# Attention by pairs of heads, scan sums formed by TensorE, and the sine products of the states on GpSimd

## The reference, cut to what matters

```python
# stick-breaking heads
z = jnp.einsum('bhqd,bhkd->bhqk', q_blk, k) * (q_blk.shape[-1] ** -0.5)
log_fail = jnp.where(earlier, jax.nn.log_sigmoid(-z), 0.0)
log_stick = lax.cumsum(log_fail, axis=3, reverse=True) - log_fail
w = jnp.where(earlier, jnp.exp(jax.nn.log_sigmoid(z) + log_stick), 0.0)
# softmax heads
p = jax.nn.softmax(jnp.where(visible, z, -jnp.inf), axis=-1)
# S5
_, _, h_re, h_im = lax.associative_scan(_complex_affine_combine,
    (lam_re, lam_im, bu_re, bu_im), axis=1)
y = einsum('bsgn,gcn->bsgc', h_re, c_re) - einsum('bsgn,gcn->bsgc', h_im, c_im)
y = jax.nn.gelu(y + d_skip * u)
```

## Time and profile before

| | us |
|---|---|
| median of 3 runs | 2449.45 (2447.01 to 2452.51) |
| the profiled execution, its own time | 2445.27 |
| its span, first to last instruction | 2443.3 |
| TensorE busy | 1999.7 (82%) |
| VectorE busy | 800.5 (33%) |
| ScalarE busy | 263.0 (11%) |
| GpSimd busy | 0.2 (0%) |

### The profile page before, as it was taken

The page is one execution under the profiler, slowest core; times in us unless marked ns, Lnnn a source line. Parts: engine busy times, 40 slices in busy tenths (PEclk is TensorE's granted clock), DMA queues, the critical chain, the costliest instruction groups (busy, mean ns, idle before and its releaser), DMA issues.

```text
span 2443.3 us, 28860 instructions
## 1 busy us (share of the span) xinstructions
PE 1999.7 (82%) x12526; PEld 1046.5 (43%) x12526; DVE 800.5 (33%) x1592; ACT 263.0 (11%) x447; POOL 0.2 (0%) x4
## 2 busy tenths in 40 slices
PE   8769675767666759589999944599999999999988
PEld 4658663222222226446767631343433433333322
DVE  1665742333333343632043377310111211121112
ACT  1221110111111110530100000000000000000000
POOL 0000000000000000000000000000000000000000
PEclk9879787887887769689999965799999999999999
DMA  6210005899999982004343200199999999999996
GB/s 241 78 65 4 2 2 210 377 430 431 431 430 432 429 357 103 0 1 190 138 172 138 104 0 0 73 429 430 404 408 405 379 430 430 431 429 429 430 431 258
DMA packets 50981, 645.06 MB, mean 264 GB/s; under 512 B 8192, under 2 KB 10496, under 8 KB 12064
## 3 DMA queue, kind: packets, MB, share of 16 engines
q1 hardware_dynamic: 50848, 643.11, 62.9%
HBM read 642.04 MB, written 1.05 MB: 263 GB/s over the span
## 4 chain that ended last, share of the span: by engine, by line
PE 69%; DVE 13%; DMA 12%; issue 4%; ACT 2%; DVEq 0%; SPq 0%; ACTq 0%
PE ps L765 67%; DMA slot<-in_moe_w_up 12%; DVE xn L1931 2%; DVE hT L1931 1%; PE ps L1308 1%; DVE hT L1935 1%; DVE xn L1972 1%; DVE xn L2929 1%; DVE sca L1931 1%; ACT L1690 1%; PE ps L774 0%; DVE x_sb L1938 0%; DVE xn L1935 0%; DVE BK L1931 0%; PE ps L914 0%
## 5 line engine op out<-in xcount | busy, mean ns | idle before, releaser
L765 PE MATMUL ps<-slot,xgT 128*32 128x512 f32 (+2 forms) x2368 | 408.3, 672 | 75.6 <-issue 41.0
L765 PE MATMUL ps<-hT,slot 128*128 128x256 f32 (+2 forms) x1536 | 316.0, 368 | 3.2 <-DVE hT L1935 3.2
L765 PEld LDWEIGHTS ps<-hT,slot 128*128 128x128 f32 (+2 forms) x1536 | 274.6, 185 | 45.9 <-DVE hT L1935 4.3
L765 PEld LDWEIGHTS ps<-slot,xgT 128*32 128x32 f32 (+2 forms) x2368 | 130.9, 133 | 345.3 <-issue 319.5
L765 PE MATMUL ps<-slot,xgh 128*64 128x512 f32 x1120 | 256.1, 600 | 4.3 <-DVE x_sb L1938 2.2
L765 PE MATMUL ps<-slot,hTs 128*64 128x512 f32 (+2 forms) x1232 | 253.5, 596 | 0.9 <-DVE hTs L2467 0.9
L765 PEld LDWEIGHTS ps<-slot,hTs 128*64 128x64 f32 (+2 forms) x1232 | 80.4, 132 | 166.6 <-issue 166.6
L765 PE MATMUL ps<-slot,hT 128*128 128x512 f32 (+1 forms) x320 | 142.3, 605 | 4.1 <-ACT hT L1690 2.3
L765 PEld LDWEIGHTS ps<-slot,xgh 128*64 128x64 f32 x1120 | 76.6, 137 | 145.9 <-issue 136.0
L765 PE MATMUL ps<-slot,hTq 128*32 128x512 f32 x512 | 93.9, 868 | 25.9 <-issue 25.4
L1931 DVE TENSOR_TENSOR hsb<-ps,sgx 64x512 f32<-64x512 f32 (+2 forms) x56 | 38.8, 693 | 232.0 <-ACT sgx L1690 141.1
(11 more groups left out here) (364 smaller groups left out, 1734.6 us busy)
## 6 DMA issues: line engine op xcount, KB each, us to landing
slot<-in_moe_w_gate SPq DMA_DIRECT2D x88, 2048.0 KB, 15.4
slot<-in_moe_w_up SPq DMA_DIRECT2D x88, 2048.0 KB, 16.7
slot<-in_moe_w_down SPq DMA_DIRECT2D x88, 2048.0 KB, 18.6
slot<-in_dffn_w_gate SPq DMA_DIRECT2D x7, 2048.0 KB, 7.7
slot<-in_dffn_w_up SPq DMA_DIRECT2D x7, 2048.0 KB, 12.5
slot<-in_dffn_w_down SPq DMA_DIRECT2D x7, 2048.0 KB, 7.7
slot<-in_w_in_tiles SPq DMA_DIRECT2D x6, 2048.0 KB, 8.5
slot<-in_att_w_in SPq DMA_DIRECT2D x3, 2048.0 KB, 12.1
```

The costliest lines, as they stand in the source:

```text
L765: return nc.tensor.matmul(o, l, r, start=start, stop=stop)
```

## The change

In attention the loop goes over four pairs of heads. The stick scores of a pair lie in two banks of a ring of their own (`sticks`, which the sums share) and are read there by ScalarE's Abs and by VectorE, without the copy. Every elementwise step of ScalarE and VectorE covers both heads, and the sums are one matmul of 512 columns and two of 256. The latent scores have a ring of two banks (`latents`). Ahead of the loop the order of the projections changes: one `sqk` bank, then the latents with `q_up` and `kv_up`, then three `sqk` banks, the stick scores of pair 0, one bank of values, the transposes of the heads, the latent scores, the second bank of values. ScalarE's copies of the values move behind `root("heads")`.

In S5 the sums of products ahead of the scans are formed by TensorE, in PSUM, by the identity and its negative (`minus`): eight logical matmuls of 128 rows by 256 columns a step. The scans read PSUM and write `scanned`. The states are multiplied by cosine on VectorE and by sine on GpSimd, and the four products of each tile go through TensorE with `cT`, and with `cN` for the negative: eight logical matmuls in place of four. The states' products of step i-1 stand behind the input products of step i on VectorE. `cN` and `minus` are made beside the dense layer by two more instructions.

```diff
+            stick_project(0)
             pe.wait_ge(lat_ready, 1)
...
+            for n in (1, 2, 3):
+                stick_project(n)
...
+            stick_scores(0)
+            values(0)
             pe.wait_ge(heads_ready, 1)
...
+            latent_scores(0)
+            values(1)
...
+            for hp in range(HP):
+                pe.wait_ge(fails, hp + 1)
+                b = sticks.claim(pe, sticks.at[f"sums{hp}"])
+                mm(b[:, :].rearrange("p (h e c) -> p h e c", h=2, e=2), cst("after"),
+                   blocks(lf)[:, :, 0::2, :]).then_inc(sticks.filled, 1)
+                b = sticks.claim(pe, sticks.at[f"sums{hp}"] + 1)
+                middle = b[:, 0:T].rearrange("p (h c) -> p h c", h=2)
+                mm(middle, cst("after"), blocks(lf)[:, :, 1, :], True, False)
+                mm(middle, cst("ones"), blocks(lf)[:, :, 2, :], False, True).then_inc(sticks.filled, 1)
+                if hp + 1 < HP:
+                    stick_scores(hp + 1)
+                    latent_scores(hp + 1)
+                pe.wait_ge(p_ready, hp + 1)
...
+            for hp in range(HP):
+                act.wait_ge(w_arg, hp + 1)
+                f(wT, la, ACT.Exp).then_inc(w_exp, 1)
+                if hp + 1 < HP:
+                    soft(hp + 1)
+                for k in range(2):
+                    empty(pair_item(f"turned{k}", hp), (pTt[:, k, :], lambda b: b[:, 0:3 * P], 1.0))
+                if hp + 1 < HP:
+                    probabilities(hp + 1)
...
+            for hp in range(HP):
+                if hp:
+                    failing(hp)
+                attempts(hp)
+                normalised(hp)
+                if hp + 1 < HP:
+                    latent_max(hp + 1)
+                dve.wait_ge(w_exp, hp + 1)
+                signal(tt(edge(wT), edge(wT), strictly, ALU.mult), w_ready, hp + 1)
...
+            def s5_turned(i):
                 for m in range(2):
+                    bu.landed(pe, bu.at[i] + m)
+                    b = rotated.claim(pe, rotated.at[i] + m)
+                    mm(b[:, 0:T], ident, vst[:, 0, m, 0, :], True, False)
+                    mm(b[:, 0:T], ident, vst[:, 1, m, 1, :], False, True)
+                    mm(b[:, T:2 * T], ident, vst[:, 0, m, 1, :], True, False)
+                    mm(b[:, T:2 * T], minus[:, :], vst[:, 1, m, 0, :], False, True).then_inc(rotated.filled, 1)
...
+            for i in range(9):
+                if i < 8:
+                    s5_turned(i)
+                if i:
+                    s5_out(i - 1)
                 if i < 6:
                     s5_in(i + 2)
...
+        @block.gpsimd
+        def _(pool):
+            for i in range(8):
+                rotated.landed(pool, rotated.at[i] + 1)
+                if i:
+                    pool.wait_ge(s5y.filled, i)
+                for m in range(2):
+                    nc.gpsimd.tensor_tensor(hsin[:, m], scanned[:, m],
+                                            rot[:, 1, 2 * i + m, :].unsqueeze(1).to_broadcast([P, 2, T]),
+                                            ALU.mult).then_inc(s5_hsin, 1)
...
+            for i in range(10):
                 if i < 8:
+                    s5_products(i)
+                if 0 < i < 9:
+                    s5_states(i - 1)
+                if i > 1:
+                    s5_outputs(i - 2)
+                if i < 8:
+                    s5_scan(i)
```

More of the change, by code:

```diff
@@ L609, in either @@
                         packed(x)
-        def scores_item(kind, h):
-            return V.at["heads"] + 3 * h + ("stick", "latent", "sums").index(kind)
         def pair_item(kind, hp):
             return S_.at["pair"] + 4 * hp + ("turned0", "turned1", "stick", "latent").index(kind)
-        def s5_item(kind, i):
-            return V.at["s5"] + (2 * i + max(i - 1, 0) if kind == "in" else (23 if i == 7 else 3 * i + 4))
         def arrived(eng, name):
@@ L1603, in _ @@
             S_.landed(pe, pair_item("latent", HP - 1))
+            sticks.landed(pe, sticks.total - 1)
+            latents.landed(pe, latents.total - 1)
             out_proj(("p0", "p1"), V.at["wout2"])
@@ new lines, in _, with latent_max @@
+            blocks = lambda x: x.rearrange("p h (b c) -> p h b c", b=3)
+            edge = lambda x: blocks(x)[:, :, 0::2, :]
+            strictly = cst("before").unsqueeze(1).unsqueeze(1).to_broadcast([P, 2, 2, P])
+            def latent_max(hp):
+                for k in range(2):
+                    b = latents.take(dve, latents.at[f"s{hp}"] + k)
+                    own(tt(mz[:, k, 0:P], b[:, 0:P], cst("causal")[:, P:2 * P], ALU.add))
+                    tt(mz[:, k, P:3 * P], b[:, P:3 * P], cst("causal"), ALU.add).then_inc(latents.emptied, 1)
+                own.settle()
+                latents.landed(dve, latents.at[f"s{hp}"] + 1)
+                own(vec.tensor_reduce(st[:, 32:34], mz[:, :, 0:P], AXX, ALU.max))
+                own(vec.tensor_reduce(st[:, 34:36], mz[:, :, P:3 * P], AXX, ALU.max))
+                own.settle()
+                signal(ts(st[:, 36:40], st[:, 32:36], -(MQK ** -0.5), ALU.mult), maxed, hp + 1)
@@ new lines, in failing @@
+            def failing(hp):
+                dve.wait_ge(z_soft, hp + 1)
+                two = [sticks.take(dve, sticks.at[f"z{hp}"] + k) for k in range(2)]
+                for k in range(2):
+                    own(stt_(lf[:, k, :], two[k][:, 0:3 * P], 0.0, sp_[:, k, :], ALU.max, ALU.add))
+                own.settle()
+                tt(edge(lf), edge(lf), strictly, ALU.mult).then_inc(fails, 1)
+                for k in range(2):
+                    stt_(la[:, k, :], two[k][:, 0:3 * P], 0.0, sp_[:, k, :], ALU.min,
+                         ALU.subtract).then_inc(sticks.emptied, 1)
@@ new lines, in s5_scan @@
+            def s5_scan(i):
+                if i:
+                    dve.wait_ge(s5_h, 2 * i)
+                    dve.wait_ge(s5_hsin, 2 * i)
+                for m in range(2):
+                    b = rotated.take(dve, rotated.at[i] + m)
+                    dec = q(3)[:, 2 * i + m:2 * i + m + 1].to_broadcast([P, T])
+                    for k in range(2):
+                        ins = vec.tensor_tensor_scan(scanned[:, m, k, :], dec, b[:, k * T:k * T + T], 0.0,
+                                                     ALU.mult, ALU.add)
+                    ins.then_inc(rotated.emptied, 1)
@@ new lines, in s5_states, with s5_outputs @@
+            def s5_states(i):
+                rotated.landed(dve, rotated.at[i] + 1)
+                if i:
+                    dve.wait_ge(s5y.filled, i)
+                for m in range(2):
+                    tt(hcos[:, m], scanned[:, m], tiled(rot[:, 0, 2 * i + m, :], 2), ALU.mult).then_inc(s5_h, 1)
+            def s5_outputs(i):
+                o, j = 64 * (i % 2), i // 2
+                b = s5y.take(dve, s5y.at[i])
+                stt_(yT[o:o + 64, j, :], uT[o:o + 64, j, :], pcol("sd", j)[o:o + 64, :], b[o:o + 64, 0:T],
+                     ALU.mult, ALU.add).then_inc(s5y.emptied, 1)
```

331 lines of the change are left out of this document (147 added, 184 removed).

## The result

The changed kernel takes 2373.43 us (median of 4 runs, 2372.51 to 2375.59), the kernel before 2450.97 in the same runs (4 runs, 2447.01 to 2452.51). The ratio is 0.9687, 95% interval [0.9671, 0.9704]: 77.5 us less. The forecast was 2376, range 2364 to 2402. The profiled span is 2370.9 us in place of 2443.3.

The account below looks back on a forecast made before the run. It took a chain across engines to bound the head loop and VectorE to bound S5. Gains of 44.5 (attention), 26.3 (S5) and 2.3 (`glu`) make 73.1: 2445.27 becomes 2372.2, plus 4.2 for the median 2376 us; range 2364 to 2402.

Parts of the forecast that it names:

- Ahead of the loop: Attention before the head pairs: latents' transposes 20.7 us earlier, TensorE then late, first `wT` exponential at 986.6 us.
- Periods of a pair: Attention loop: 11.0 us a pair in place of 17.1, between 10.2 and 11.9 by the clock.
- Tail: End of attention: last pair's mask, transposes, weighting and copies to the output projection take 6.0 us.
- `glu`: Projection behind S5: entered at full clock, it falls from 30.18 to 27.8 us, 2.3 us gained.
- S5's gain: S5 stage: steps of 7.2 us in place of 10.88, the stage 62.3 in place of 88.6, 26.3 us gained.
- The sine product: GpSimd in S5: 1.2 us for each product of 512 columns, bounds 0.62 and 2.4, covered up to 1.95.
- Rival (a): S5 scans: TensorE stays at 1.2 GHz, 2417 us, or about 2396 for half the steps; chance 0.16 whole or half.
- Rival (b): S5: VectorE and GpSimd hold each other up, 2392 us, or 2378 if only cosine products wait; chance 0.14.
- Rival (c): Attention: pairs do not do what they say, a pair stays at 13.5 us, 2385 us; chance 0.12.
- Rival (d): S5: a sine product takes 8 us, 2472 us, slower than before; decides from 7.1 us a product; chance 0.02.
- A gain passes through: Behind attention and S5: nothing waits for a fixed time, so what either stage loses, the span loses.
- the forecast's own ends: Whole kernel: 2370 us with periods of 10.2 and steps of 6.7, and 2384 us at the other end.

Follow-up runs that it names:

- experiment 3: Changed kernel with all four stick banks projected ahead of the latents again, pairs kept: 2390.95 us, ratio 0.9762.
- experiment 6: Changed kernel with the sums ahead of the S5 scans made by VectorE in SBUF in place of TensorE: 2381.15 us, ratio 0.9719.
- experiment 8: Changed kernel with GpSimd writing zeros of the same size in place of the sine products: 2368.05 us, one run.
- experiment 7: Changed kernel with each sine product made twice on GpSimd, once into unused memory: 2390.98 us, one run.
- experiment 10: Changed kernel with the second bank of values behind the first sums and the last S5 sine product on VectorE: 2371.8 us, ratio 0.9683.
- experiments 1: Kernel before with the attention part of the change alone, S5 as before: 2401.41 us, ratio 0.9808.
- experiment 5: Changed kernel with the sine products on VectorE and GpSimd idle: 2378.57 us, ratio 0.9711.

## Why the prediction was right, step by step

The time was forecast to 2.6 us, and the mechanisms that it rests on are in the trace: the chain ahead of the heads, the pairs, full clock in S5, and gains that pass through. The terms were off by up to 4.5 us for attention. The agreement of the profiled spans (72.4 us apart, 73.1 forecast) is better than the sum was, by luck: from the first stick projection to the first expert weights 76.8 us were gained, 3.7 more than forecast, and this execution came to that projection 3.35 later.

- **Ahead of the loop: right.** Measured from the first stick projection, the root stands at 26.8 us (forecast 26.6), the heads' transposes at 47.0 (47.2), the first sums at 60.9 (62.0), the first `wT` exponential at 63.9 (65.3). That TensorE and no longer the chain of the heads would be late there was right, and experiment 3 gives its price, 17.5 us.
- **Periods of a pair: 11.0 forecast, 10.5 measured** (31.6 us for three). I had added for the lower clock, since the earlier trace rows show 0.70. With pairs the loop's clock is 0.91. The addition was not wrong in kind: in the third period, 10.10 us, the weighting runs at full clock (1.5 us from start to end), and in the second, 10.88, at the lower level (2.8), with the sums behind it. The period is set by the cycle across the engines and not by ScalarE's own work, which I had also put at 10.2: ScalarE is busy for 9.3 us of the second period and waits 1.6 for VectorE's subtraction.
- **Tail: 6.0 forecast, 4.3 measured** (1020.17 to 1024.45); how much of this the clock gives is not settled. The start of the loop, the periods and the tail make 49.0 in place of 44.5, and all three were put too long.
- **What the clock gives and takes behind the changed stages.** `glu` gained 2.45 us (forecast 2.3), but the forecast let it pass to the end, and the router gave 1.5 back. The output projection gained 1.3 and the `u` projection lost 2.2, neither of them forecast.
- **S5's gain: 26.3 forecast, 27.3 measured, from two errors that cancel in part.** The step is 6.70, not 7.2: of the 0.4 us for signals nothing is seen, as the products of the next step need nothing from the scans just issued and follow them without a gap. The scans from PSUM cost what they did from SBUF (664 ns each, four in 2.42 us: 2.44). The part behind the last scans is 7.6 us, not 5.6. I had laid sine, output and skip term end to end as if GpSimd were alone; but the last cosine and sine products start together and take turns (3.44 us for the sine pair, not 2.50), and TensorE, which has waited 4.0 us, runs the output matmuls at the lower level (4 in 1.13 us, which took 0.60 in the steps ahead).
- **The sine product: 1.2 us forecast, 1.27 measured.** By the Trainium skill (GPSIMD Engine Reference, section 3.1) the estimate was 1.12; the trace shows 13% more.
- **Rival (a), the lower clock in the scans: no.** 1.00 for most of S5; and experiment 6 shows 0.64 with the sums taken away from TensorE.
- **Rival (b), VectorE and GpSimd hold each other up: its small form is true, and I had priced it about right.** I wrote that the cosine products would wait for the sine products under way and that this costs 2 us. It is in every cosine row above 0.69 us, and by experiment 8 it is 0.19 us a step, 1.3 in seven, to which the last step adds 0.9 on the sine pair. The clearest rows are the last step's two cosine products:

```profile
L2006 DVE TENSOR_TENSOR hT<-dense_part,rot x2: 691/1222/1752, 1437.2 to 1437.8; 128x512 f32<-128x512 f32 x2
```

The first takes 0.69 us; the first sine product, started 0.05 later, takes 1.77, since it waits for it; the second cosine product takes 1.75. The Trainium skill (SBUF — State Buffer, "Who interferes with whom") says that a VectorE instruction with two SBUF inputs contends with a GpSimd one that reads SBUF, but not with one that only writes it, and that one with a single SBUF input does not contend. The traces agree on all three: cosine products of 914 ns in the mean beside sine products, a cosine pair of 1.29 us beside the memsets, and input products of 674 ns beside sine products (experiment 8). It also calls the shared ports an exclusive lock, and the turns of whole instructions in experiments 7 and 10 bear that out. What I did not do was to apply the rule to the last step, where the two have no other work between them.
- **Rival (c), pairs that bring nothing: no**, by experiments 1 and 3. **Rival (d), a sine product of 8 us: no**, it is 1.27; the size from which it would have decided is, by its own sum (23.5 us too many at 8 us, 16 for each us), some 6.5 us and not 7.1.
- **A gain passes through: right, but for the router's 1.5.** The first expert weights were forecast near 1503 and are issued at 1502.65, by the luck named above; the stages behind keep their length to 1.05 us.

The range was wider than needed, since the doubt on the clock did not come true. The upper one of the forecast's own ends, 2384, does not follow from the bounds given, periods of 11.9 and steps of 8.5 us, which make 2388.

## What to carry to other kernels

A loop in which no engine is full can gain from doing two items per turn, since table loads and signals are paid once for both. Price it from the cycle across the engines as well as from the fullest engine's own work (here the cycle was the longer one), and look up at which of the two clock levels its matmuls run. Sums that VectorE would form in SBUF can go to TensorE through PSUM by an identity. Here that was worth 7.7 us, since TensorE had room for them and the clock was 1.00 with them and 0.64 without. In this kernel work on GpSimd that reads SBUF cost nothing only while VectorE read one operand from SBUF beside it: lay it beside such work, start it as soon as that work starts, and look at the last turn of the loop, in which there is none.

## What the runs showed of the hardware

- VectorE and GpSimd, both reading two SBUF operands, go turn by turn, by whole instructions; the one that waits stands as busy in the trace (0.95 to 1.75 us for 0.68, 1.59 to 1.77 for 1.27). A long row of such products is then a wait, and not a slow operation.
- Mean clock and the time of the next stage are two things: with 0.64 in S5 the `glu` projection took 27.73 us (experiment 6), and with 1.00 in the steps of S5 29.67 (experiment 5), 29.41 (experiment 7) and 29.28 (experiment 10). The earlier trace rows had 30.18 with 0.52. TensorE's wait ahead of the last output matmuls does not order them either: 3.99 us and 27.73 in the changed kernel, 3.58 and 29.67 in experiment 5. What does is open.
- A stage of mostly narrow matmuls can run at full clock: of the 40 instructions of an S5 step 24 go into 32 columns or come from 32 rows, and it ran at 1.00.
